# Shared expert's down product in fourths in the last four pairs, an accumulator that starts as the scaled residual, and one expert matrix loaded ahead into x's buffer

## What is computed

```python
def moe_ffn(x, router_w, router_bias, w1, w3, w2, sw1, sw3, sw2):
    shared = (jax.nn.silu(xf @ sw1) * (xf @ sw3)) @ sw2
    ...
    routed = grouped_experts(xf, eidx, gates, w1, w3, w2)
    return (shared + routed).reshape(bsz, s_len, d)

x = layer_norm(ALPHA * x + h, ln1_g[i], ln1_b[i])
m = moe_ffn(x, ...)
x = layer_norm(ALPHA * x + m, ln2_g[i], ln2_b[i])
```

## Time and profile before

| | |
|---|---|
| median of 3 executions | 1374.41 us |
| lowest and highest | 1374.24 and 1377.72 us |
| the profiled execution | 1377.61 us |
| its span, first to last instruction | 1375.8 us |
| TensorE's mean granted clock | 0.997 |
| busy: PE, weight loads, DVE, ACT, POOL | 97%, 59%, 35%, 25%, 6% |
| DMA, mean over the span | 336 GB/s |
| layer 0's expert loop, first gate matmul to last down's start | 179.8 to 645.6 us |
| layer 1's expert loop, the same | 862.1 to 1327.7 us |

### The profile page before, as it was taken

How to read it: one execution, slowest core, us unless ns; L and a number is a source line. 1 busy time by engine, 2 the same in 40 slices (tenths; PEclk the granted TensorE clock), 3 DMA queues, 4 the chain that set the end, 5 groups by cost and what they waited for, 6 DMA issues and landing times.

```text
span 1375.8 us, 21061 instructions
## 1 busy us (share of the span) xinstructions
PE 1333.8 (97%) x8658; PEld 813.5 (59%) x8658; DVE 474.7 (35%) x791; ACT 346.6 (25%) x873; POOL 84.8 (6%) x99
## 2 busy tenths in 40 slices
PE   8999999999999999999999999999999999999998
PEld 4555765565665655555497558556566565555543
DVE  1484623232332323234501146132323323232354
ACT  1243322222222222222210223322222222222212
POOL 2443100000000000000100022000000000000000
PEclk9999999999999999999999999999999999999999
DMA  9821559999999999999754424799999999999991
GB/s 302 298 93 62 214 223 386 421 421 422 420 421 421 421 420 421 421 420 394 235 204 171 194 95 184 294 387 421 420 421 420 421 421 421 421 421 421 420 374 63
DMA packets 79861, 461.85 MB, mean 336 GB/s; under 512 B 6432, under 2 KB 6656, under 8 KB 30112
## 3 DMA queue, kind: packets, MB, share of 16 engines
q1 hardware_dynamic: 77184, 452.06, 80.9%
q0 software_dynamic: 2592, 8.53, 2.0%
HBM read 459.52 MB, written 1.05 MB: 335 GB/s over the span
## 4 chain that ended last, share of the span: by engine, by line
PE 73%; DMA 19%; DVE 6%; issue 1%; ACT 1%; DVEq 0%; SPq 0%; ACTq 0%
PE ps L1090 25%; DMA ring<-in_exp_w_dram 19%; PE ps L1118 11%; PE ps L1138 7%; PE ps L762 4%; PE ps L1252 4%; DVE o_tok L1934 3%; PE ps L866 3%; PE ps L950 3%; PE ps L1010 2%; PE ps L974 2%; PE ps L632 1%; PE ps L1002 1%; PE ps L935 1%; PE ps L782 1%
## 5 line engine op out<-in xcount | busy, mean ns | idle before, releaser
L1118 PE MATMUL ps<-ring,qkT 128*64 128x512 f32 x1024 | 233.9, 599 | 0.0
L1934 DVE TENSOR_TENSOR o_tok<-ps,o_tok 128x1024 f32<-128x1024 f32 x124 | 151.9, 1225 | 87.3 <-PE ps L1138 86.2
L1940 DVE TENSOR_TENSOR y_lo<-ps,y_hi 128x1024 fp32r<-128x1024 f32 x62 | 75.9, 1225 | 233.4 <-ACT y_hi L1478 233.4
L1924 DVE SCALAR_TENSOR_TENSOR roped<-roped,rows,ps 128x256 f32<-128x256 f32 x64 | 30.8, 481 | 331.0 <-ACT roped L1451 319.4
L1118 PEld LDWEIGHTS ps<-ring,qkT 128*64 128x64 f32 x1024 | 67.8, 136 | 111.8 <-issue 110.4
L1090 PE MATMUL ps<-ring,xT 128*64 128x256 f32 x1024 | 122.3, 381 | 9.3 <-DMA ring<-in_exp_w_dram 9.0
L1090 PE MATMUL ps<-ring,pT 128*64 128x256 f32 x1024 | 121.9, 380 | 4.3 <-DMA ring<-in_exp_w_dram 4.3
L1478 ACT ACTIVATE y_hi<-ps 128x1024 fp32r<-128x1024 f32 x62 | 63.5, 1024 | 240.5 <-PE ps L1118 240.5
L1090 PE MATMUL ps<-ring,proj 128*64 128x256 f32 x1024 | 121.6, 379 | 0.0
L1090 PE MATMUL ps<-ring,gb_row 128*64 128x256 f32 x1024 | 121.4, 379 | 0.0
L1138 PE MATMUL ps<-y_hi,selT 128*128 128x512 f32 x248 | 111.1, 448 | 10.2 <-DVE o_tok L1934 8.7
(11 more groups left out here) (276 smaller groups left out, 1508.9 us busy)
## 6 DMA issues: line engine op xcount, KB each, us to landing
ring<-in_exp_w_dram SPq DMA_DIRECT2D x178, 2048.0 KB, 19.9
ring<-in_exp_w_dram SPq DMA_DIRECT2D x24, 1024.0 KB, 6.9
ring<-in_od_w_in_dram SPq DMA_DIRECT2D x6, 2048.0 KB, 8.5
ring<-in_ple_w_gate_dram SPq DMA_DIRECT2D x4, 2048.0 KB, 15.4
ring<-in_ev_w_in_dram SPq DMA_DIRECT2D x3, 2048.0 KB, 19.9
ring<-in_ev_w_o_dram SPq DMA_DIRECT2D x2, 2048.0 KB, 10.0
ring<-in_exp_w_dram SPq DMA_DIRECT2D x8, 512.0 KB, 19.3
ring<-in_od_w_o_dram SPq DMA_DIRECT2D x2, 2048.0 KB, 8.0
```

What stands on the lines that cost most here:

```text
L1118: ins = pe.matmul(ps[b * SLOTS:(b + 1) * SLOTS, 4 + half, :], hT[:, f, b * SLOTS:(b + 1) * SLOTS], views[b][:, f, half * PIECE:(half + 1) ...
L1924: dve.scalar_tensor_tensor(h_exp, h_silu, slot_gate[:, par:par + 1], ps[:, 2, FE:2 * FE], ALU.mult, ALU.mult)\
L1934: dve.tensor_tensor(y_acc[:, t, :], ps[:, bank:bank + 2, :].rearrange("p b n -> p (b n)"), y_acc[:, t, :], ALU.add)\
L1940: dve.tensor_tensor(y_lo[:, :], ps[:, 4:6, :].rearrange("p b n -> p (b n)"), y_hi[:, :], ALU.subtract)\
```

## The change

- The shared down product is cut into fourths, q = 0 to 3 (token tile q // 2, column half q % 2). Fourth q runs in pair 28 + q between its gate and its up matmuls, into PSUM bank 1; DVE adds it to `y_acc` (`add_shared`) ahead of the pair's product. `shared_add` and the work in pairs 0 and 1 are gone.
- `y_acc` is begun by ACT as ALPHA times `x_tok` (`y_begin`), ahead of the loop. `add_residual` is gone.
- The shared expert's third matrix goes into pT and its second into `small`, `selbias` and `tmp_o`, four DMAs behind the wait for the last attention products.
- `x_tok` is free in the loop. Expert 4's first (gate) matrix is loaded into it ahead of the loop (`extra_load`), pair 2 reads it from there, and the first pair load brings only expert 5's first matrix.
- SP's pair loads of the first round stand outside its loop. The overflow path takes x from its two split parts.

```diff
--- before.py
+++ after.py
@@ -200,8 +200,10 @@
             return (xe_odd if odd else xe_even)[c // 4][:, c % 4:c % 4 + 2, :]
 
         shared_w1 = qkT[:, 0:DC, :]
-        shared_w3 = o_tok[:, :, :].rearrange("p t n -> p (t n)").rearrange("p (c f) -> p c f", c=DC)
-        shared_w2 = proj_flat[:, NT * D:2 * NT * D].rearrange("p (f n) -> p f n", f=2)
+        shared_w3 = pT[:, :, :].rearrange("p a n -> p (a n)").rearrange("p (c f) -> p c f", c=DC)
+        selbias_flat = selbias[:, :, :].rearrange("p t n -> p (t n)")
+        shared_w2 = ((small[:, 0:PIECE], small[:, PIECE:D]), (selbias_flat, tmp_o))
+        extra_w1 = x_tok[:, :, :].rearrange("p t n -> p (t n)").rearrange("p (c f) -> p c f", c=DC)
         h_silu = roped[:, 0, 1536:1792]
         h_exp = roped[:, 0, 1792:2048]
         slot_gate = rows[:, 492:494]
@@ -407,13 +409,19 @@
                 units = FIRST_UNIT[L] + len(UNITS[L % 2])
                 sp.wait_ge(sem("sc_mm"), units)
                 sp.dma_start(shared_w1, a["sh_w1"][L].rearrange("(p c) f -> p c f", c=DC)).then_inc(sem("shared_w1_loaded"), 16)
-                if L == 0:
-                    sp.wait_ge(sem("qkT_tp"), len(QKT_BATCHES))
-                else:
-                    sp.wait_ge(sem(f"ple_out{L - 1}"), 2 * NT)
+                sp.wait_ge(sem("pv_mm"), units)
                 sp.dma_start(shared_w3, a["sh_w3"][L].rearrange("(p c) f -> p c f", c=DC)).then_inc(sem("shared_w3_loaded"), 16)
-                sp.wait_ge(sem("pv_mm"), units)
-                sp.dma_start(shared_w2, a["sh_w2"][L].rearrange("(p f) n -> p f n", f=2)).then_inc(sem("shared_w2_loaded"), 16)
+                rows_f = a["sh_w2"][L].rearrange("(p f) n -> p f n", f=2)
+                sp.dma_start(small[:, 0:D], rows_f[:, 0, :]).then_inc(sem("shared_w2_loaded"), 16)
+                for half in range(2):
+                    sp.dma_start(shared_w2[1][half], rows_f[:, 1, half * PIECE:(half + 1) * PIECE]).then_inc(sem("shared_w2_loaded"), 16)
+
+            def extra_load(L):
+
+                sp.wait_ge(sem("router_mm"), NT * (L + 1))
+                sp.wait_ge(sem("x_split"), NT * (L + 1))
+                sp.wait_ge(sem("y_begun"), NT * (L + 1))
+                sp.dma_start(extra_w1, a["exp_w1"][L, RING].rearrange("(p c) f -> p c f", c=DC)).then_inc(sem("extra_loaded"), 16)
 
             def over_load(L, e):
                 up = rows_of
@@ -441,8 +449,12 @@
                             e = i * UNROLL + u
                             two = slice(e, e + 2) if isinstance(i, int) else bass.ds(e, 2)
                             sp.wait_ge(sem("exp_gate"), i * 2 + (L * PAIRS + u // 2 - 1))
-                            sp.dma_start(two_slots(s, 0, UP_N), a["exp_w1"][L, two].rearrange("e (p c) f -> p e (c f)", c=DC))\
-                              .then_inc(w1_loaded[s], 16)
+                            if isinstance(i, int) and e == RING:
+                                sp.dma_start(ring[:, (s + 1) % RING, 0:UP_N], a["exp_w1"][L, e + 1].rearrange(rows_of, c=DC))\
+                                  .then_inc(w1_loaded[s], 16)
+                            else:
+                                sp.dma_start(two_slots(s, 0, UP_N), a["exp_w1"][L, two].rearrange("e (p c) f -> p e (c f)", c=DC))\
+                                  .then_inc(w1_loaded[s], 16)
                             sp.wait_ge(sem("exp_up"), i * 2 + (L * PAIRS + u // 2 - 1))
                             sp.dma_start(two_slots(s, UP_N, 2 * UP_N), a["exp_w3"][L, two].rearrange("e (p c) f -> p e (c f)", c=DC))\
                               .then_inc(w_loaded[s], 16)
@@ -458,7 +470,10 @@
                                     sp.dma_start(w2[:, :, cols], a["exp_w2"][L, e + b].rearrange("(p c) f -> p c f", c=2)[:, :, cols])\
                                       .then_inc(down_loaded[(s + half) % RING], 16)
 
-                        with sp.Fori(1, NE // UNROLL - 1) as i:
+                        extra_load(L)
+                        for u in range(0, UNROLL, 2):
+                            pair_load(1, u)
+                        with sp.Fori(2, NE // UNROLL - 1) as i:
                             for u in range(0, UNROLL, 2):
                                 pair_load(i, u)
                         pair_load(NE // UNROLL - 1, 0)
@@ -1003,6 +1018,19 @@
                                             w2[:, f, half * PIECE:(half + 1) * PIECE], start=(f == 0), stop=(f == 1))
                     return ins
 
+                def shared_down(q, L=L):
+
+                    t, half = q // 2, q % 2
+                    if q == 0:
+                        pe.wait_ge(sem("shared_w2_loaded"), 48 * (L + 1))
+                        pe.wait_ge(sem("shared_h"), NT * (L + 1))
+                    else:
+                        pe.wait_ge(sem("y_added"), 2 * (L * PAIRS + PAIRS - 5 + q))
+                    for f in range(2):
+                        ins = pe.matmul(ps[:, 1, :], h_all[:, f * SEQ + t * P:f * SEQ + (t + 1) * P], shared_w2[f][half],
+                                        start=(f == 0), stop=(f == 1))
+                    ins.then_inc(sem("shared_down"), 1)
+
                 def shared_up(t, blocks):
 
                     for n in blocks:
@@ -1010,17 +1038,6 @@
                             ins = pe.matmul(ps[:, 4 + t, n * P:(n + 1) * P], (shared_w1, shared_w3)[n // 2][:, c, n % 2::2],
                                             xT[:, c, t * P:(t + 1) * P], start=(c == 0), stop=(c == DC - 1))
                     return ins
-
-                def shared_down(t, L=L):
-
-                    if t == 0:
-                        pe.wait_ge(sem("shared_w2_loaded"), 16 * (L + 1))
-                        pe.wait_ge(sem("shared_h"), NT * (L + 1))
-                        bank = 6
-                    else:
-                        pe.wait_ge(sem("xe_copied"), 4 * L * OCTETS + 5)
-                        bank = 0
-                    down_tile(shared_w2, t, bank).then_inc(sem("shared_down"), 1)
 
                 pe.wait_ge(sem("shared_w1_loaded"), 16 * (L + 1))
                 shared_up(0, (0, 1))
@@ -1076,7 +1093,12 @@
 
                         pe.wait_ge(sem("exp_h"), m + M0)
                     views = [ffn_views((ks + 1 + 2 * par + b) % RING) for b in range(2)]
+                    if m == RING // 2:
+                        views[0] = (extra_w1, *views[0][1:])
+                        pe.wait_ge(sem("extra_loaded"), 16 * (L + 1))
                     for w in range(2):
+                        if w == 1 and m >= PAIRS - 4:
+                            shared_down(m - (PAIRS - 4))
                         for b in range(2 if m < 2 else 1):
                             k = ks + 1 + 2 * par + b
                             if w == 0:
@@ -1126,10 +1148,9 @@
 
                     if t == 0:
                         pe.wait_ge(sem("y_split"), m + (M0 + 1))
-                    if isinstance(m, int) and m == 0 and t == 0:
-                        pe.wait_ge(sem("shared_added"), NT * L + 1)
                     if bank == 0:
                         pe.wait_ge(sem("y_added"), 2 * m + 2 * M0)
+                        pe.wait_ge(sem("shared_added"), 4 * L + m - (PAIRS - 6))
                     elif not (first and t == 0):
 
                         pe.wait_ge(sem("y_added"), 2 * m + (2 * M0 + t))
@@ -1145,14 +1166,10 @@
 
                     par = u % 2
                     exp_up(m, o, odd, u, par, first and M0 == 0)
-                    if isinstance(m, int) and m < NT:
-                        shared_down(m)
                     if scatter_last:
                         scatter(m - 1, 0, 1 - par, M0 == 0 and isinstance(m, int) and m == 1)
                     if gather_next:
                         pe.wait_ge(sem("xe_copied"), 4 * o + (4 * O0 + 4 + u))
-                        if m == 1:
-                            pe.wait_ge(sem("shared_added"), NT * (L + 1))
                         gather(o + 1, u, halves=(0, 1) if scatter_last else (0,))
                     h_transpose(m)
                     if gather_next and not scatter_last:
...
@@ -1410,19 +1430,19 @@
                     act.wait_ge(sem("router_mm"), NT * L + t + 1)
                     act.activation(sig[:, t, :], ps[:, 6 + t, 0:NE], ACT.Exp, scale=-1.0).then_inc(sem("router_e"), 1)
 
-                def shared_add(t):
-                    act.wait_ge(sem("shared_down"), NT * L + t + 1)
-                    bank = 0 if t else 6
-                    act.activation(y_acc[:, t, :], ps[:, bank:bank + 2, :], ACT.Copy).then_inc(sem("shared_added"), 1)
+                def y_begin(t):
+                    act.activation(y_acc[:, t, :], x_tok[:, t, :], ACT.Copy, scale=ALPHA).then_inc(sem("y_begun"), 1)
 
                 rsqrt_guess()
                 x_high(0)
                 copy_T("xT_act", tp, 0)
                 router_exp(0)
+                y_begin(0)
                 rsqrt_guess()
                 x_high(1)
                 copy_T("xT_act", tp, 1)
                 router_exp(1)
```

(26 more changed lines are left out.)

## The result

The changed kernel takes 1377.91 us (median of 20 executions, 1376.01 to 1380.65), the one before 1376.84 us in its 20 executions of the same series: ratio 1.0015, 95% interval 1.0009 to 1.0021. No gain but a loss of 1.1 us, and 10 us above the forecast of 1367.8. The profiled execution took 1377.91 us, its span is 1376.1 us (1375.8 before).

What follows compares the result with a forecast made beforehand. The stream of expert weights was taken to bound the loop's end once gapless; 5.7 us gained less 2.4 for the fourths gives 3.3 a layer, 6.6 in two, 1374.41 to 1367.8 us, range 1362.5 to 1375.5.

Steps and rivals of the forecast that it cites:

- C: Start of the loop: the stream gains nothing and the fourths still cost; 4.8 us lost, 1379.2 us; chance 0.10.
- D: Last four pairs: nothing is absorbed, the fourths cost 7.3 us a layer; 3.2 us lost, 1377.6 us; chance 0.06.
- (1): Pairs 0 and 1 without the shared down: 2.85 and 3.55 us less, together 6.4 us at pair 1's down.
- (2): Expert weight stream: earlier issues behind the first pairs' downs make it gapless sooner; it gains 5.7 us a layer.
- Rival B: Loop start: a hole before pair 1's transfer, or no extra-matrix share; net 1.5 us a layer, 1371.4 us; chance 0.20.
- (3): Expert 4's first matrix, loaded ahead of the loop into a DMA hole: 1.0 of the stream's 5.7 us a layer.
- rival E: Ahead of the loop: the extra matrix does nothing, its 1.0 us being inside a hole; 1369.8 us; chance 0.05.
- (4): Last four pairs: the fourths, partly absorbed by waits for the stream, cost 2.4 us a layer; bounds 0 to 7.3.
- Rival A: Last four pairs: the fourths are filled in whole by PE's waits; gain 11.4 us, 1363.0 us; chance 0.12.
- (5): Last four pairs: DVE adds each fourth in 0.68 us, done 2.5 us before the product's silu arrives: free.
- (6): Residual start on ACT ahead of the loop: takes 1.0 us, bounds 0 to 2.11; 0 on the path.
- (7): Shared weights before the loop: third matrix issued later, four DMA issues of about 2 us on SP; costs nothing.

Runs made afterwards that it cites:

- kernel 1: The changed kernel, but the overflow path transposes `x_tok` again (16 transposes instead of 32 matmuls on the split parts); 1370.60 us, ratio 0.9963.
- kernel 2: The kernel before, with only the overflow path's 16 transposes replaced by 32 matmuls on the split parts; 1384.36 us, ratio 1.0055.
- kernel 4: kernel 1 without `extra_load`, so the first pair load brings both gate matrices; 1373.19 us, ratio 0.9978 to the kernel before.
- kernel 8: The changed kernel with VectorE rebuilding `x_tok` on overflow for 16 transposes, and the fourths in pairs 24 to 27 instead of 28 to 31; 1365.67 us, ratio 0.9923.

## Why the prediction was wrong

**The step that failed** is none of the seven: it is an item of the change that had no step. "The overflow path takes x from its two split parts" stands in the diff, and since the path does not run, I gave it no line in the sum, neither a price nor bounds. It cost 6.7 to 7.3 us by the changed kernel and kernel 1, and 8.1 us alone (1384.36 - 1376.23, kernel 2), more than everything else brought (5.6 us). In the trace it is the standstill of 5.15 us behind layer 0's loop and the slower product behind it, 6.4 us. None of the rivals A to E has this mechanism; C's and D's sizes, 1379.2 and 1377.6 us, lie near the result only by chance: their signs (pair 27's up no earlier; waits gone because the stream is early) are not in the trace. The sentence on what would make it wrong looked at the loop alone, and the range left the tail of a layer out.

**(1) Pairs 0 and 1:** right. Pair 0's down starts 9.4 us behind the loop's start (12.4 before), pair 1's 23.7 (30.2): 6.5 us, forecast 6.4.

**(2) The stream:** right, too small in size. It gained 6.4 us a layer, forecast 5.7: all of what the pairs gave came through, and the 0.7 us that I had held back as a remaining hole did not (kernel 1 has 6.0 in layer 0 and 6.4 in layer 1). Rival B fell with it, and C too. But B's sign, as it was worded, did come: a hole of over 1 us within 5 to 20 us of the loop's start.

```profile
188.00:190.00 2.00, 1.62 (x12) 1.19 (x14) 0.32 (x1) 0.99 (x2) 0.00 (x0) 1.00 0.58 119
195.00:196.00 1.00, 1.00 (x12) 0.68 (x10) 0.59 (x1) 0.25 (x2) 0.00 (x0) 1.00 0.64 197
```

The first of these lies between the halved load and the up transfer, ahead of pair 0's down, where step (3) itself leaves holes. It cost nothing, so that sign could not tell B from the forecast. The figure of the Trainium skill's page "DMA: Bandwidth & Descriptors" (Bandwidth), 6.15 us for a transfer of 1 MB issued from GpSimd, by which the gain would have been 5.1 (an estimate), is the farther one. The trace disagrees with it here too: the halved load landed 4.6 us behind its issue.

**(3) The extra matrix:** right for both layers together, 1.7 us by the two loops and 2.6 by the medians (kernel 4) against 2.0 forecast, so rival E is out. One layer showed 0.1 and the other 1.6, for which step (3) has no reason.

**(4) The fourths:** the mechanism is right, the size small. 3.2 us a layer at pair 31's up, forecast 2.4. I took 1.83 us from half of the old shared down; alone between other products a fourth takes 1.92 to 2.0 (589.28 to 591.20), and the ups follow 15.20 us apart, where I had 14.96. Late by 2.3 at pair 28 (591.20 - 574.01 - 14.9), and by 0.3 more (15.20 - 14.9) in each of the next three. Rival A (filled in whole) is ruled out by the rows without a wait, D by the 3.2 us.

**(5) VectorE's additions, (6) the start on ScalarE, (7) the shared weights:** free as forecast. From layer 0's last down to layer 1's loop, where (6) and (7) lie for layer 1, kernel 1 and the kernel before both take 216.5 us. The addition took 0.69 us (0.68 in the earlier trace rows) and the start 1.05 us (1.0 taken, bounds 0 to 2.11):

```profile
591.37 0.69 DVE L1966 TENSOR_TENSOR o_tok<-ps,o_tok 128x512 f32<-128x512 f32 x1 [3.98 <-PE ps L1030]
```

```profile
168.39 1.05 ACT L1434 ACTIVATE o_tok<-x_tok 128x1024 f32<-128x1024 f32 x1
```

**The sum:** 6.4 - 3.2 = 3.2 us a layer against 3.3 forecast: two errors of 0.7 to 0.8 us that cancel, so that the near match is luck. Over both layers 6.4 us, and 5.6 by kernel 1. Without the longer branch the forecast would have missed by 2.8 us in absolute terms; 1.8 of these are the baseline, since the kernel before stands at 1376.2 where more executions are taken, and not at 1374.41.

## What to carry to other kernels

An item of a diff that is never executed still has a length: it moves all code behind it, and a jump over it may land in a block that is not there. So price it, bounds 0 and the nearest hole with the releaser "issue", and look at every jump ahead of work that nothing else hides. If such a hole shows up, a shorter path, the work on another engine's path, or another number of instructions ahead of the jump can take it away; the number has to be measured, since here 160 more took the hole away while 32 and 64 more made two of it. And in this loop, which waits for a stream, the extra work was best placed ahead of the shortest pairs, not into them: their spare time then paid for it after the fact (kernel 8).

## What the runs showed of the hardware that was not expected

A jump of TensorE over 299 instructions cost 5.1 to 5.5 us in six of twelve places, 0.8 and 2.0 us in two, nothing in four; a jump over 203 cost nothing in twelve cases. In a full hole 2.4 to 2.9 us pass up to the packet of 16.3 KB and 2.6 to 2.8 us behind it. In the six full holes the granted clock also falls from 2.4 to 1.2 GHz, and the product behind them took 8.5 to 10.1 us instead of 7.0, 1.5 to 3.1 us more, which comes on top. Executions scatter more where the jump starts near a border: 10.2 us between the lowest and the highest of ten with the two short holes, against 4.5 us in the ten of kernel 4, which has no hole. And without any hole, between the two loops, a fall of the granted clock cost 1.6 us in five of the twelve traces.
